# A two-layer hybrid decoder on one core: the experts' results added to the rows of x by an adding indirect DMA, weights split a whole expert ahead, no combine

## The chip, the core and the metric

The kernel runs on one core of one Trainium2 chip. A core has the engines TensorE (PE), VectorE (DVE), ScalarE (ACT), GpSimd (POOL) and SyncE (SP), an on-chip memory of 128 partitions, the matrix engine's accumulators (PSUM, 8 banks), and 16 DMA engines that move data between the chip's main memory (DRAM) and the on-chip memory. Each engine works through its own list of instructions and waits for others by semaphores. The metric is the device time of one execution in microseconds (us).

## The reference

A token is a row of 1024 numbers, and there are 2048 of them. Layer 0 mixes tokens by gated linear attention, layer 1 by a recurrent block. After each mixer comes the mixture of experts, which is what the change is about:

```python
def hier_moe(x, norm_w, w_group, w_expert, w_gate, w_up, w_down):
    h = rmsnorm(x, norm_w).reshape(n_tok, d)
    # best group of 4, then the best 2 of its 8 experts; weights of the two
    ...
    weights = p_g[:, None] * top_p
    eid = g_sel[:, None] * MOE_EXPERTS_PER_GROUP + top_e
    ...
    def expert_block(args):        # a block: up to 128 rows of one expert
        xblk, e = args
        return (jax.nn.silu(xblk @ w_gate[e]) * (xblk @ w_up[e])) @ w_down[e]
    yb = lax.map(expert_block, (xb, blk_eid)).reshape(n_rows, d)
    yb = yb * buf_w[:, None].astype(yb.dtype)
    out = jnp.zeros((n_tok + 1, d), yb.dtype).at[buf_tok].add(yb)[:n_tok]

def reference(x, ...):
    for layer in range(DEPTH):
        x = x + gla_mixer(...)  if layer % 2 == 0 else x + rglru_mixer(...)
        x = x + hier_moe(...)
    return rmsnorm(x, final_norm)
```

There are 32 experts of size 1024 x 256 (gate), 1024 x 256 (up) and 256 x 1024 (down), all fp32, so 3 MB of weights for each expert and layer.

## The kernel before

The program runs seven stages one after the other, with a barrier between them: `gla` (mixer of layer 0), `project_and_route` (output projection, residual, norm, choice of experts), `experts`, `lru` (mixer of layer 1), `project_and_route`, `experts`, `finish` (last norm).

Every large product is made of three matmuls in a 32-bit format with a shorter mantissa (`matmul3`, L118 to L120): the operands are split into a high part (`hi`, made by a copy on ACT) and a low part (`lo`, raw minus high, a subtraction of two operands on DVE or POOL). So each weight of each expert has to be split before PE can use it.

**Routing** writes for every pair of token and chosen expert the token's number into `gather_lists` by an indirect DMA (L920). It keeps the pair's weight (`k.weight`) and, after the last tile, computes at which row of `y_rows` the pair's result will stand (`k.row`, L1097 to L1103).

**Experts** walks over 32 experts, and for each over its blocks of 128 rows (`expert_blocks`). The counts are data: an expert has 1 or 2 blocks here, once 3. All engines walk the same loops. For block g, of expert e:

- POOL gathers the rows of the *next* block from `h_rows` by one indirect DMA of 512 KB (`gather`, L1274 and L1277), once the rows of block g have been transposed.
- PE multiplies by gate and up (24 matmuls of 512 columns, `experts_gu`), transposes the next block's rows (L1411), does the down product of the block *before* (`down`, 12 matmuls), and transposes the activations (L1446).
- ACT takes silu (L1346), then `hT_hi` of the next rows (L1316), y of the block before (L1323), `aT_hi` (L1350), and stores y to `y_rows` by a plain DMA (L1328).
- DVE does act = silu x up (L1397), `hT_lo` (L1386) and `aT_lo` (L1400).

Between experts stands the splitting of weights, in two slots of raw, hi and lo. At the head of expert e, ACT makes `gu_hi` of expert e+1 (L1309, 3/8 and 5/8 apart), DVE makes `wd_hi` and `wd_lo` of expert e (L1375, L1377) and 3/8 of `gu_lo` of expert e+1 (L1366), and POOL makes the other 5/8 of `gu_lo`, of expert e itself (L1285). SP loads gate and up of expert e+2 when both parts of `gu_lo` of e are done, and down of e+2 when `wd_lo` of e is done (L1241).

**The combine** stands in the stage behind. `lru` (before its norm) and `finish` gather for each of 16 tiles of tokens two rows of `y_rows` per token by indirect DMAs, `y_a` and `y_b` (L1647; L1477), and DVE adds them to x with their weights in two instructions (L1763, L1765; L1494, L1496). `lru` stores the new x again (L1589). Its SP queue holds in this order: x of tiles 0 and 1, gain, weights, store of x 0, x 2, more weights, eight small loads of parameters (L1606, L1608), then store and load of the further tiles. During `gla`, POOL sets the unused part of `y_rows` to zero by 8 DMAs of 2 MB (L418).

## Time and profile before

| | us |
|---|---|
| median of 3 runs (3321.96 to 3325.31) | 3324.17 |
| the profiled execution | 3325.53 |
| its span in the trace | 3324.0 |
| `gla` and first routing, 0 to 1156 | 1156 |
| `experts` of layer 0, 1156 to 1767 | 611 |
| `lru`, 1767 to 2338 | 571 |
| second routing, 2338 to 2619 | 281 |
| `experts` of layer 1, 2619 to 3202 | 583 |
| `finish`, 3202 to 3324 | 122 |

The stages were cut where SP issues the first load of the next one. The trace gives for each engine when an instruction ran and what ended the engine's idle time before it. The granted clock is TensorE's, 1.00 for 2.4 GHz and 0.50 for 1.2 GHz. A DMA's landing time runs from its issue to its completion.

### The profile page before, as it was taken

To read this page: it belongs to the slowest core of one execution; us is meant where nothing else is said; L and a number is where in the kernel's file an instruction comes from. 1 tells how busy PE (TensorE), PEld (TensorE's weight loads), DVE (VectorE), ACT (ScalarE), POOL (GpSimd) and SP (SyncE) were. 2 spreads that over 40 slices of the span, in tenths; PEclk is the share of its full clock that TensorE was granted. 3 is DMA by queue.
4 is the path that set the end of the run, shared out by engine and by line. 5 is a ranking of instruction groups with operands and counts; after the bars stand their busy time and mean duration, and the time that the engine had idled before them with its cause. 6 is when DMAs were issued, how large, how long until landed. Compare 5 with 4: busy or idle time off the path is not lost. (4 is left out here: it accounts for less than half of the span.)

```text
span 3324.0 us, 46214 instructions
## 1 busy us (share of the span) xinstructions
PE 2699.6 (81%) x12218; PEld 2149.8 (65%) x12219; DVE 1897.1 (57%) x3349; ACT 1505.0 (45%) x2058; POOL 706.0 (21%) x458
## 2 busy tenths in 40 slices
PE   4999969999699577988883999998799378999840
PEld 3777747777587466766762877776577356777630
DVE  3444434444366567456554788876466687544745
ACT  3444544455344244444443676675344344444423
POOL 0000000000011245344441010000011354344532
PEclk8999979999899789999996999999899698999975
DMA  3122212222444287777757455431543487777757
GB/s 109 64 70 70 76 63 70 70 76 76 151 146 132 87 284 272 266 256 259 263 197 235 147 181 161 144 120 51 191 136 126 160 294 278 263 264 252 265 205 256
DMA packets 360028, 563.86 MB, mean 170 GB/s; under 512 B 30608, under 2 KB 272416, under 8 KB 359968
## 3 DMA queue, kind: packets, MB, share of 16 engines
q1 hardware_dynamic: 314080, 402.11, 37.1%
q0 software_dynamic: 29616, 101.76, 9.1%
q10 hardware_dynamic: 16272, 59.25, 4.4%
q8 instruction: 30, 0.49, 0.1%
q14 instruction: 30, 0.25, 0.0%
HBM read 427.77 MB, written 135.30 MB: 169 GB/s over the span
## 5 line engine op out<-in xcount | busy, mean ns | idle before, releaser
L1285 POOL TENSOR_TENSOR experts_gu_lo<-experts_gu_raw,experts_gu_hi x64 | 385.6, 6025 | 160.5 <-ACT experts_gu_hi L1309 159.9
L118 PE MATMUL experts_ps<-experts_gu_hi,experts_hT_hi 128*128 (+1 forms) x760 | 331.8, 437 | 91.4 <-issue 71.3
L119 PE MATMUL experts_ps<-experts_gu_lo,experts_hT_hi 128*128 (+1 forms) x760 | 319.7, 421 | 0.0
L120 PE MATMUL experts_ps<-experts_gu_hi,experts_hT_lo 128*128 (+1 forms) x760 | 318.0, 418 | 0.0
L1366 DVE TENSOR_TENSOR experts_gu_lo<-experts_gu_raw,experts_gu_hi (+1 forms) x64 | 279.7, 4371 | 67.0 <-ACT experts_gu_hi L1309 67.0
L1309 ACT ACTIVATE experts_gu_hi<-experts_gu_raw (+1 forms) x128 | 238.0, 1908 | 91.3 <-DMA experts_gu_raw<-in_moe_w_up 32.1
L118 PE MATMUL route_ps<-route_w_hi,route_src_hi 128*128 128x512 f32 x512 | 215.1, 420 | 56.8 <-DVE route_w_lo L979 56.8
L118 PEld LDWEIGHTS experts_ps<-experts_gu_hi,experts_hT_hi 128*128 128x128 f32 x760 | 156.1, 205 | 141.0 <-issue 106.9
L118 PE MATMUL gla_ps<-gla_wvg_hi,gla_hT_hi 128*128 128x512 f32 x512 | 212.6, 415 | 0.0
L120 PE MATMUL route_ps<-route_w_hi,route_src_lo 128*128 128x512 f32 x512 | 208.7, 408 | 0.0
L119 PE MATMUL route_ps<-route_w_lo,route_src_hi 128*128 128x512 f32 x512 | 208.6, 407 | 0.0
L120 PE MATMUL gla_ps<-gla_wvg_hi,gla_hT_lo 128*128 128x512 f32 x512 | 202.5, 395 | 0.0
L119 PE MATMUL gla_ps<-gla_wvg_lo,gla_hT_hi 128*128 128x512 f32 x512 | 201.2, 393 | 0.0
L1323 ACT ACTIVATE experts_y<-experts_ps 128x1024 f32<-128x1024 f32 x97 | 99.6, 1026 | 179.2 <-PE experts_ps L120 162.9
L120 PEld LDWEIGHTS experts_ps<-experts_gu_hi,experts_hT_lo 128*128 128x128 f32 x760 | 155.0, 204 | 38.7
L119 PEld LDWEIGHTS experts_ps<-experts_gu_lo,experts_hT_hi 128*128 128x128 f32 x760 | 156.3, 206 | 33.9
L418 POOL DMA_DIRECT2D y_rows<-gla_zeros x8 | 9.2, 1146 | 787.0 <-DVE gla_tile_decay L629 787.0
L1346 ACT ACTIVATE experts_silu<-experts_ps 128x256 f32<-128x256 f32 x95 | 36.4, 383 | 292.1 <-PE experts_ps L120 290.5
L920 POOL DMA_INDIRECT gather_lists<-route_tok,route_place_int x64 | 61.8, 965 | 489.7 <-DVE route_place_int L1049 480.0
L118 PE MATMUL experts_ps<-experts_wd_hi,experts_aT_hi 128*128 (+1 forms) x388 | 161.6, 417 | 3.4 <-DVE experts_aT_lo L1400 3.4
L1411 PE MATMUL experts_ps<-ident,experts_rows 128*128 128x128 f32 x776 | 104.5, 278 | 66.6 <-DMA experts_rows<-h_rows,experts_ids_now 66.1
L119 PE MATMUL experts_ps<-experts_wd_lo,experts_aT_hi 128*128 (+1 forms) x388 | 153.3, 395 | 0.0
(311 smaller groups left out, 6571.4 us busy)
## 6 DMA issues: line engine op xcount, KB each, us to landing
experts_gu_raw<-in_moe_w_gate SPq DMA_DIRECT2D x64, 1024.0 KB, 5.7
experts_gu_raw<-in_moe_w_up SPq DMA_DIRECT2D x64, 1024.0 KB, 10.8
experts_wd_raw<-in_moe_w_down SPq DMA_DIRECT2D x64, 1024.0 KB
y_rows<-experts_y ACTq DMA_DIRECT2D x97, 512.0 KB, 6.3
gla_w_raw<-in_gla_w_in SPq DMA_DIRECT2D x18, 1024.0 KB
y_rows<-gla_zeros POOLq DMA_DIRECT2D x8, 2048.0 KB, 8.4
route_src<-oT_rows SPq DMA_DIRECT2D x32, 512.0 KB, 4.3
x_rows<-route_x_new SPq DMA_DIRECT2D x32, 512.0 KB, 2.9
```

The costliest lines, as they stand in the source:

```text
L118: nc.tensor.matmul(out, w_hi, x_hi, start=first, stop=False)
L119: nc.tensor.matmul(out, w_hi, x_lo, start=False, stop=False)
L120: return nc.tensor.matmul(out, w_lo, x_hi, start=False, stop=last)
L418: pool.dma_start(y_unused[bass.ds(n * rows, rows), :] .rearrange("(p n) (a c) -> p (n a) c", p=P, c=DV), zeros[:].unsqueeze(1).to_broadcas ...
L920: pool.indirect_dma_start(ids_out, bass.IndirectOffsetOnAxis(place_int[:, j, c:c + 1].bitcast(U32), 0), tok[:, j:j + 1], None).then_inc(sc ...
L1285: pool.tensor_tensor(gu_lo[:, slot(e), DVE_SHARE:], gu_raw[:, slot(e), DVE_SHARE:], gu_hi[:, slot(e), DVE_SHARE:].bitcast(F32), ALU.subtract)\
L1309: nc.scalar.activation(gu_hi[:, slot(e), at], gu_raw[:, slot(e), at], ACT.Copy)\
L1323: nc.scalar.activation(y[:].rearrange("p (b c) -> p b c", b=2), ps[:, Y:Y + 2], ACT.Copy)\
L1346: nc.scalar.activation(silu[:], ps[:, GU, 0:FF], ACT.Silu).then_inc(silu_done, 1)
L1366: nc.vector.tensor_tensor(gu_lo[:, slot(e), 0:DVE_SHARE], gu_raw[:, slot(e), 0:DVE_SHARE], gu_hi[:, slot(e), 0:DVE_SHARE].bitcast(F32), AL ...
L1411: last = nc.tensor.transpose(ps[:, HT_ + c // 4, (c % 4) * P:(c % 4 + 1) * P], rows[:, c * P:(c + 1) * P], k.ident[:])
```

## The change

Routing now writes entries of two numbers, the token and its weight (`entry`), into `expert_lists`. Empty places hold the numbers T to T+127, which are spare rows at the end of x. `k.row`, `k.weight` and the instructions behind them are gone, h is stored as two halves of 512 columns, and the zeroing in `gla` is gone.

In `experts` POOL splits no weights any more. DVE subtracts all of `gu_lo` of expert e+1, in four parts of 128 x 1024 that follow four parts of `gu_hi` on ACT, and `wd_lo`; ACT makes `wd_hi` too, once the down product before has ended. The rows of a block come in two gathers of 512 columns, each transposed between halves of the gate-and-up product. y is multiplied by its weight when ACT takes it from PSUM, and POOL adds it to the rows of x in DRAM by an indirect DMA with an addition (`add_y`); the next y, in the same single buffer, waits for that DMA to have landed. ACT's order within a block is now aT, y, half of hT, silu, half of hT. y has two blocks of delay to its gather, and the pipeline is filled by two dummy blocks of zeros. `lru` and `finish` read the finished x; their gathers, their combine and `lru`'s stores of x are gone.

```diff
@@ experts, POOL
             def gather(column, g):
-                pool.wait_ge(hT_ps_done, nth(g - 1))
+                for b in range(2):
+                    if not (isinstance(g, int) and g == 0):
+                        pool.wait_ge(rows_in[b], nth_dma(g - 1))
+                    stand(pool)
+                    pool.tensor_copy(source_now[b][:], sources[:, bass.ds(column, 1)]).then_inc(source_set[b], 1)
+                    pool.wait_ge(source_set[b], nth(g))
+                    pool.wait_ge(hT_ps_done, nth(2 * g - 2 + b))
+                    stand(pool)
+                    pool.indirect_dma_start(rows[:, b], None, h_halves[b],
+                                            bass.IndirectOffsetOnAxis(source_now[b][:].bitcast(U32), 0))\
+                        .then_inc(rows_in[b], DMA)
...
+            def add_y(i):
+                if not (isinstance(i, int) and i < 0):
+                    pool.wait_ge(y_added, nth_added(i - 1))
+                pool.wait_ge(listed, nth(i - 2))
                 stand(pool)
+                pool.tensor_copy(target_now[:].unsqueeze(1), by_block[:, bass.ds(i + (LAG - 2), 1), 0:1])\
+                    .then_inc(target_set, 1)
+                pool.wait_ge(target_set, nth(i + 1))
+                pool.wait_ge(y_done, nth(i))
                 stand(pool)
+                pool.indirect_dma_start(x_rows, bass.IndirectOffsetOnAxis(target_now[:].bitcast(U32), 0),
+                                        y[:], None, compute_op=ALU.add).then_inc(y_added, DMA)
-            def split_gu(e):
-                pool.wait_ge(gu_hi_done, nth(2 * e))
-                pool.tensor_tensor(gu_lo[:, slot(e), DVE_SHARE:], gu_raw[:, slot(e), DVE_SHARE:],
-                                   gu_hi[:, slot(e), DVE_SHARE:].bitcast(F32), ALU.subtract)\
-                    .then_inc(gu_lo2_done, 1)
@@ experts, ACT
+            def take_y(i):
+                act.wait_ge(y_ps_done, nth(i))
+                act.wait_ge(y_added, nth_added(i - 1))
+                act.wait_ge(listed, nth(i - 2))
+                stand(act)
+                nc.scalar.activation(y[:].rearrange("p (b c) -> p b c", b=2), ps[:, Y:Y + 2], ACT.Copy,
+                                     scale=by_block[:, bass.ds(i + (LAG - 2), 1), 1].bitcast(F32))\
+                    .then_inc(y_done, 1)
...
+            def before(e, first):
+                if not is_last(e):
+                    split_gu(e + 1)
+                split_wd(e, first)
             def each(e, b, g):
+                take_aT(g)
+                take_y(g)
+                take_rows(g + 1, 0)
                 act.wait_ge(gu_ps_done, nth(g))
                 act.wait_ge(act_done, nth(g - 1))
                 nc.scalar.activation(silu[:], ps[:, GU, 0:FF], ACT.Silu).then_inc(silu_done, 1)
-                take_rows(g + 1)
-                take_y(g)
-                act.wait_ge(aT_ps_done, nth(g))
-                nc.scalar.activation(aT_hi[:], ps[:, AT, 0:FF].rearrange("p (a c) -> p a c", c=P), ACT.Copy)\
-                    .then_inc(aT_hi_done, 1)
-                store_y(g)
+                take_rows(g + 1, 1)
@@ experts, PE
             def each(e, b, g):
-                pe.wait_ge(gu_lo_done, nth(e))
-                pe.wait_ge(gu_lo2_done, nth(e))
-                pe.wait_ge(hT_lo_done, nth(g))
                 pe.wait_ge(act_done, nth(g - 1))
...
+                for half in range(2):
+                    pe.wait_ge(hT_lo_done, nth(2 * g + half))
+                    for c in range(KD)[of_half(half)]:
+                        if c % PK == 0:
+                            pe.wait_ge(gu_lo_done, nth(PARTS * e + c // PK))
+                        last = matmul3(nc, ps[:, GU], hT_hi[:, c], hT_lo[:, c], gu_hi[:, slot(e), c],
+                                       gu_lo[:, slot(e), c], c == 0, c == KD - 1)
+                    if half == 1:
+                        last.then_inc(gu_ps_done, 1)
+                    transpose_rows(g + 1, half)
@@ lru (finish in the same way)
-            def combine(t):
-                j = t % 2
-                after_dma(dve, x_in[j], t // 2)
-                after_dma(dve, y_in[j], 2 * (t // 2) + 1)
-                step(nc.vector.scalar_tensor_tensor(out=x[:, j], in0=y_a[:, j], scalar=k.weight[:, t, 0:1],
-                                                    in1=x[:, j], op0=ALU.mult, op1=ALU.add))
-                nc.vector.scalar_tensor_tensor(out=x[:, j], in0=y_b[:, j], scalar=k.weight[:, t, 1:2],
-                                               in1=x[:, j], op0=ALU.mult, op1=ALU.add).then_inc(x_done, 1)
```

POOL's list in the loop over experts (experts 0 to 30), in the kernel before: first what stands once per expert, then one block, whose loop is closed by L1216.

```order
L1285 TENSOR_TENSOR experts_gu_lo<-experts_gu_raw,experts_gu_hi 128x2560
...
L1214 TENSOR_LOAD block_at
...
L1215 TENSOR_LOAD blocks
...
L1274 COPY experts_ids_now<-experts_ids 128x1
...
L1277 DMA experts_rows<-h_rows,experts_ids_now 128x1024
L1216 REGISTER_ALU
L1216 COMPARE_AND_BRANCH
```

The same place in the changed kernel:

```order
L1194 TENSOR_LOAD block_at
...
L1195 TENSOR_LOAD blocks
...
L1267 COPY experts_source_now<-experts_sources 128x1
...
L1271 DMA experts_rows<-h_rows,experts_source_now 128x512
L1267 COPY experts_source_now<-experts_sources 128x1
...
L1271 DMA experts_rows<-h_rows,experts_source_now 128x512
...
L1275 COPY experts_by_block<-experts_lists 128x2
...
L1282 COPY experts_target_now<-experts_by_block 128x1
...
L1287 DMA x_rows<-experts_y,experts_target_now 2176x1024
```

The subtraction of weights has left POOL. A block now has three DMAs and four small copies there in place of one and one, and the adding DMA stands behind both gathers.

ACT's list in the same loop, in the kernel before, with the weights of the next expert first and one block behind them:

```order
L1309 ACTIVATE experts_gu_hi<-experts_gu_raw 128x2560
...
L1309 ACTIVATE experts_gu_hi<-experts_gu_raw 128x1536
...
L1346 ACTIVATE experts_silu<-experts_ps 128x256
...
L1316 ACTIVATE experts_hT_hi<-experts_ps 128x512 x2
...
L1323 ACTIVATE experts_y<-experts_ps 128x1024
L1350 ACTIVATE experts_aT_hi<-experts_ps 128x256
...
L1328 DMA y_rows<-experts_y 128x1024
```

The same place in the changed kernel, from the last of the four parts of `gu_hi` on:

```order
L1335 ACTIVATE experts_gu_hi<-experts_gu_raw 128x1024
...
L1342 ACTIVATE experts_wd_hi<-experts_wd_raw 128x2048
...
L1318 ACTIVATE experts_aT_hi<-experts_ps 128x256
...
L1326 ACTIVATE experts_y<-experts_ps,experts_by_block 128x1024
...
L1313 ACTIVATE experts_hT_hi<-experts_ps 128x512
...
L1363 ACTIVATE experts_silu<-experts_ps 128x256
...
L1313 ACTIVATE experts_hT_hi<-experts_ps 128x512
```

`wd_hi` has come to ACT, the store of y has left it, and y is taken ahead of silu.

## Rows read from the trace of the kernel before

**Rows 1.** Stretches: each engine's busy us (instructions), granted clock, DMA share, GB/s.
```profile
1156.00:1767.00 611.00, 510.07 (x2274) 402.00 (x2274) 348.43 (x294) 258.32 (x314) 271.30 (x134) 0.92 0.73 251
1767.00:2338.00 571.00, 478.51 (x2048) 382.32 (x2048) 426.98 (x472) 345.44 (x391) 49.14 (x50) 0.92 0.46 149
```

**Rows 2.** Timeline of ACT: start and length in us of each block's silu.
```profile
1185.37 0.38 ACT L1346 ACTIVATE experts_silu<-experts_ps 128x256 f32<-128x256 f32 x1 [1.46 <-PE experts_ps L120]
1194.85 0.38 ACT L1346 ACTIVATE experts_silu<-experts_ps 128x256 f32<-128x256 f32 x1 [4.48 <-PE experts_ps L120]
...
1224.59 0.38 ACT L1346 ACTIVATE experts_silu<-experts_ps 128x256 f32<-128x256 f32 x1
1243.37 0.38 ACT L1346 ACTIVATE experts_silu<-experts_ps 128x256 f32<-128x256 f32 x1 [6.04 <-PE experts_ps L120]
...
1754.31 0.38 ACT L1346 ACTIVATE experts_silu<-experts_ps 128x256 f32<-128x256 f32 x1 [4.49 <-PE experts_ps L120]
...
2649.22 0.39 ACT L1346 ACTIVATE experts_silu<-experts_ps 128x256 f32<-128x256 f32 x1 [1.90 <-PE experts_ps L120]
...
3151.16 0.38 ACT L1346 ACTIVATE experts_silu<-experts_ps 128x256 f32<-128x256 f32 x1 [0.21 <-PE experts_ps L120]
3169.28 0.38 ACT L1346 ACTIVATE experts_silu<-experts_ps 128x256 f32<-128x256 f32 x1 [5.46 <-PE experts_ps L120]
...
3188.25 0.38 ACT L1346 ACTIVATE experts_silu<-experts_ps 128x256 f32<-128x256 f32 x1 [4.50 <-PE experts_ps L120]
```

**Rows 3.** Timeline inside one long interval, on POOL, DVE and PE.
```profile
1223.49 6.26 POOL L1285 TENSOR_TENSOR experts_gu_lo<-experts_gu_raw,experts_gu_hi  x1 [5.30 <-ACT experts_gu_hi L1309]
1229.70 1.71 POOL L1274 COPY experts_ids_now<-experts_ids 128x1 int32 x1
1232.20 0.98 POOL L1277 DMA_INDIRECT experts_rows<-h_rows,experts_ids_now  x1 [0.79 <-POOL experts_ids_now L1274]
...
1224.72 6.65 DVE L1366 TENSOR_TENSOR experts_gu_lo<-experts_gu_raw,experts_gu_hi  x1 [0.49 <-ACT experts_gu_hi L1309]
...
1235.09 0.79 PE L118 MATMUL experts_ps<-experts_gu_hi,experts_hT_hi 128*128 x1 [2.89 <-issue]
```

**Rows 4.** Timeline, one `gu_lo` on DVE; then groups of 1156 to 1767.
```profile
1331.63 1.76 DVE L1366 TENSOR_TENSOR experts_gu_lo<-experts_gu_raw,experts_gu_hi  x1 [0.37 <-ACT experts_gu_hi L1309]
...
L1309 ACT ACTIVATE experts_gu_hi<-experts_gu_raw x62 | 115.3, 1908 | 41.1 <-DMA experts_gu_raw<-in_moe_w_gate 16.0 <-issue 15.3 <-DMA experts_gu_raw<-in_moe_w_up 9.8
L1377 DVE TENSOR_TENSOR experts_wd_lo<-experts_wd_raw,experts_wd_hi x31 | 71.1, 2293 | 3.8
```

**Rows 5.** DMA of 1156 to 1767: queues with share, then issues, us to landing.
```profile
q1 hardware_dynamic: 75408, 100.93, 50.2%
q0 software_dynamic: 7200, 26.22, 12.5%
q10 hardware_dynamic: 7200, 26.22, 10.5%
...
y_rows<-experts_y ACTq DMA_DIRECT2D x50, 512.0 KB, 6.2
experts_rows<-h_rows,experts_ids_now POOLq DMA_INDIRECT x50, 7.5
```

**Rows 6.** Timeline of `lru`: load of x 3, first large matmul.
```profile
1805.60 0.34 SPq L1585 DMA_DIRECT2D lru_x<-x_rows  x1
...
1821.91 0.80 PE L118 MATMUL lru_ps<-lru_hT_hi,lru_wx_hi 128*128 128x512 f32 x1 [4.29 <-DVE lru_hT_lo L1779]
```

**Rows 7.** Timeline of `finish`: from one tile to the next.
```profile
3281.68 0.16 DVE L1491 COPY finish_weight_now<-weight 128x2 f32 x1
...
3284.60 1.06 ACT L247 ACTIVATE finish_square<-finish_x 128x1024 f32<-128x1024 f32 x1 [4.35 <-DVE finish_x L1496]
...
3290.48 1.06 ACT L247 ACTIVATE finish_square<-finish_x 128x1024 f32<-128x1024 f32 x1 [4.35 <-DVE finish_x L1496]
```

**Rows 8.** One tile's view in `lru`: ns min/median/max of the gather's issue.
```profile
L1647 POOL DMA_INDIRECT lru_y_a<-y_rows,lru_row_now x16: 957/1833/1842, 1768.4 to 2110.7; - x16
```

More of the change, by code:

```diff
@@ L1295, in next_rows @@
                     gather(nc.s_assert_within(column, min_val=0, max_val=E * SLOTS - 1), g + 1)
+                    add_y(g)
                 return next_rows
             gather(0, 0)
-            blocks = expert_blocks(pool, None, split_gu, each)
-            pool.wait_ge(rows_in, nth_dma(blocks))
+            add_y(-1)
+            blocks = expert_blocks(pool, None, None, each)
+            for i in range(2):
+                add_y(blocks + i)
+            for b in range(2):
+                pool.wait_ge(rows_in[b], nth_dma(blocks))
@@ L1320, in take_y @@
-            def take_y(g):
-                act.wait_ge(y_ps_done, nth(g))
-                act.wait_ge(y_stored, nth_store(g - 1))
-                nc.scalar.activation(y[:].rearrange("p (b c) -> p b c", b=2), ps[:, Y:Y + 2], ACT.Copy)\
-                    .then_inc(y_done, 1)
-            def store_y(g):
-                act.wait_ge(y_done, nth(g))
-                act.dma_start(y_rows[bass.ds(g * P, P), :], y[:]).then_inc(y_stored, DMA)
+                for c in range(PARTS):
+                    stand(act)
+                    nc.scalar.activation(gu_hi[:, slot(e), of_part(c)], gu_raw[:, slot(e), of_part(c)], ACT.Copy)\
+                        .then_inc(gu_hi_done, 1)
@@ L1330, in _, with split_wd @@
+            def split_wd(e, first):
+                act.wait_ge(wd_in, nth_dma(e))
+                act.wait_ge(y_ps_done, nth(first))
+                stand(act)
+                nc.scalar.activation(wd_hi[:, slot(e)], wd_raw[:, slot(e)], ACT.Copy).then_inc(wd_hi_done, 1)
             act.wait_ge(zeroed, 1)
@@ L1403, in _ @@
-            expert_blocks(dve, each, before)
+                take_rows(g + 1, 1)
+            blocks = expert_blocks(dve, each, before)
+            take_aT(blocks)
         @block.tensor
         def _(pe):
-            def transpose_rows(g):
-                pe.wait_ge(rows_in, nth_dma(g))
-                pe.wait_ge(hT_lo_done, nth(g - 1))
-                for c in range(KD):
-                    last = nc.tensor.transpose(ps[:, HT_ + c // 4, (c % 4) * P:(c % 4 + 1) * P],
-                                               rows[:, c * P:(c + 1) * P], k.ident[:])
-                last.then_inc(hT_ps_done, 1)
@@ L1431, in each @@
+            down(0, 1)
+            transpose_act(0)
             def each(e, b, g):
-                pe.wait_ge(gu_lo_done, nth(e))
-                pe.wait_ge(gu_lo2_done, nth(e))
-                pe.wait_ge(hT_lo_done, nth(g))
                 pe.wait_ge(act_done, nth(g - 1))
-                for c in range(KD):
-                    last = matmul3(nc, ps[:, GU], hT_hi[:, c], hT_lo[:, c], gu_hi[:, slot(e), c],
-                                   gu_lo[:, slot(e), c], c == 0, c == KD - 1)
-                last.then_inc(gu_ps_done, 1)
@@ L1636, in _ @@
             after_dma(sp, y_stored, STEPS - 1)
-            for j in range(2):
-                after_dma(sp, x_stored[j], NT // 2 - 1)
-        @block.gpsimd
-        def _(pool):
-            for t in range(NT):
-                after(pool, x_done, t - 2)
-                pool.tensor_copy(row_now[:, t % 2], k.row[:, t]).then_inc(row_set, 1)
-                after(pool, row_set, t)
-                for c, rows in enumerate((y_a, y_b)):
-                    pool.indirect_dma_start(rows[:, t % 2], None, y_rows,
-                                            bass.IndirectOffsetOnAxis(row_now[:, t % 2, c:c + 1].bitcast(U32), 0))\
-                        .then_inc(y_in[t % 2], DMA)
         @block.scalar
@@ L1657, in mean_square @@
             def mean_square(t):
-                after(act, x_done, t)
+                after_dma(act, x_in[t % 2], t // 2)
                 after(act, std_done, t - 1)
@@ L1922, in lru, with finish @@
         m.end()
-def finish(nc, k, x_dram, y_rows, norm_w, out):
+def finish(nc, k, x_dram, norm_w, out):
     DEPTH = 4
@@ L1932, in finish @@
         square = m.sb("square", [P, D])
-        y_a, y_b = m.sb("y_a", [P, DEPTH, D]), m.sb("y_b", [P, DEPTH, D])
-        cb = Combine(m, k, x, h, square[:], y_a, y_b, DEPTH)
+        norm = Norm(m, k, x, h, square[:], DEPTH)
+        x_in = [m.plain(f"x_in{j}") for j in range(DEPTH)]
         stored = [m.store(f"stored{j}") for j in range(DEPTH)]
```

380 lines of the change are left out of this document (165 added, 215 removed).

## Prediction

> **What bounds the kernel now.** I read the stretches first, one per stage, because the bound differs from stage to stage. In `experts` of layer 0 PE is busy 510 of 611 us and DMA 0.73 of the time; in `lru` PE is busy 479 of 571 [rows 1]. So both wait mainly for PE, and the question is where PE loses its rest. The next view is the timeline of ACT's silu, which comes once per block and so ticks the blocks. The 49 blocks of layer 0 and the 46 of layer 1 make 48 + 45 = 93 intervals, of together 568.9 + 539.0 = 1108.0 us [rows 2]. Inside an expert of two blocks an interval is 9.48 us. But 22 intervals (11 in each layer, the first 18.78 us, the last 18.12 us) take 399.3 us together, 18.15 each; the other 71 have a mean of 9.98 [rows 2].
>
> The timeline inside one long interval shows why. POOL's part of `gu_lo` takes 6.26 us and DVE's 6.65 us, both at once, where DVE alone needs 1.76 us for the same [rows 3, 4]. DVE's act for PE is queued behind that instruction, and so are `hT_lo` and `aT_lo`. PE starts the next block after another 2.89 us of idle, with a matmul of 0.79 us, a length that stands where the granted clock is 0.50 [rows 3]. It happens behind an expert of one block, when the weights of two experts are split close together. Layer 0 has 15 such experts and layer 1 has 19 (counted from silus between two `gu_hi`).
>
> **The change part by part**, against the profiled execution's 3325.5 us (1.4 above the median).
>
> *The port stalls go.* POOL subtracts no more, so the 22 long intervals lose their cause. What is late next in a block of an expert of one block is DVE or ACT. DVE: `gu_lo` is twice the size of `wd_lo`, 4.6 us, plus 2.3 for `wd_lo` [rows 4], plus what a block costs it, some 2 us (act, `aT_lo`, `hT_lo`; estimated from ACT's 2.8 below, which has y in it), is 8.9. ACT: two instructions of 1.91 for `gu_hi`, half of them again for `wd_hi`, 5.7 in all; a block costs (258.3 - 32 x 3.8) / 49 = 2.8 us; together 8.5 [rows 1, 4]. Each has about ten waits and two register loads around that. I take 10.4 us for such a block and 9.7 for the others, where PE sets the pace. With 34 blocks of experts of one block and 59 other intervals this floor is 34 x 10.4 + 59 x 9.7 = 926 us, 182 less than 1108.
>
> *A new loop of waits comes.* y has one buffer. ACT may take the next y only when the adding DMA of the last has landed, and POOL may issue that only when ACT has written y. Queued behind ACT's wait are half of hT, silu and the other half of hT; behind POOL's wait are both gathers of the next block. So a block can't be shorter than landing time L of the adding DMA, plus y on ACT (1.0, half as many columns as a mean `gu_hi` of 1.91 [rows 4]) and the semaphores between (0.6). Nothing in the trace is an adding DMA. From below, L is at least that of the plain store of y, 6.2 us, plus 0.6 for POOL's longer issue: 6.8. From above it is a gather and a store in series, 7.5 + 6.2 - 0.3 = 13.4 [rows 5]. I take **9.0**, nearer to the store, because it moves the same rows to the same memory and the read in front is spread over 16 engines and pipelined row by row; the gather, which is a read with POOL's issue, is only 0.7 above the store so counted. Then the loop is 10.6 us, for every block.
>
> In experts of one block DVE is busy nearly throughout with two-input subtractions. POOL's copy took 1.71 us behind one of them [rows 3], for one number per partition, and a gather's issue took 1.83 us at the median against 0.96 at the least while DVE was busy in `lru` [rows 8]. I add 1.0 us to the loop there: 11.6. The blocks then take 34 x 11.6 + 59 x 10.6 = 1020 us, **88 less**. With L = 6.8 the floor holds, 182 less; with 13.4 they take 34 x 16.0 + 59 x 15.0 = 1429, 321 more. Each us of L is 93 us of time.
>
> *DMA.* Per layer the queues hold the 16 engines for 0.502 + 0.125 + 0.105 = 0.732 of 611 us, 447 us [rows 5]. The store of y (64 us) becomes the add. If its read of x costs as much again it is 511 us of a stage that I expect to last some 570. That is under the stage, so the sum takes nothing for it beyond L. The Trainium skill, "Collectives: The Full Stack", section "The bandwidth ceiling", says that an add in the DMA engines runs at half the rate of a copy, for the two reads and not for the addition. By that rule the 64 us double, as in the bound above; no row here shows it.
>
> *The rows in halves.* Two issues and two copies more on POOL, about 6.2 us of POOL per block, inside 10.6: three times an issue of 0.98, 0.79 before it [rows 3] and a copy of some 0.2, and one copy more. The first half can start when half of the rows is transposed. The waits for rows that lengthen some of the 71 ordinary intervals go; they are inside the 9.7 above. Cost nothing, hidden by the loop; if POOL falls behind, see the rivals.
>
> *Head and tail of `experts`.* Two more POOL fills, a list of twice the size and a dummy add delay the first gather; the 6 us of DVE beside POOL at the head go. I take +2 each (-5 to +6). At the end the stage runs 12.7 us from the last silu at 1754.31 to 1767 [rows 1, 2], with one store. Now the last y but one can stand one loop after silu, and the last y a second, shorter one (the engines' queues empty, L some 6.5), and its add lands 6.5 later: 9 + 8 + 6, 10 more, or less where the loop isn't full: +9 each (+6 to +14). Both layers: **+22**.
>
> *`lru`.* The first large matmul starts at 1821.91, 54 us into the stage. It waits for tile 3, whose x was issued only at 1805.60 [rows 6], as SP waited with the store of x 1 behind eight small loads, and tile 0 waited for its two gathers. Now x 0 lands some 5 us into the stage, h of tile 0 is there about 10 us earlier, SP goes through the small loads 14 us earlier, and DVE saves two combines of 2.6 behind x 3: **-18** (-10 to -25). In the steady part DVE loses 2.6 us in 11 of 16 steps, but PE sets the pace there, so 0 (bound: -22, the time in which PE waited for `hT_lo`).
>
> *`finish`.* A tile takes 3290.48 - 3284.60 = 5.88 us, a serial chain over DVE and ACT. The combine in it lasts from 3281.68 to 3284.60, 2.92 us [rows 7]. What replaces it is ACT's own issue of the output before the next square, 0.6 us. So 3.6 us per tile, 15 times 2.3 is 34 less; the start loses the two gathers and one combine, about 12 less, and the end 3 less: **-49** (-40 to -56). DMA then moves 1 MB in 3.6 us, 290 GB/s, more than the mean of 251 in `experts` [rows 1], so a little may come back.
>
> *Routing and `gla`.* The row computation at its end (3 us of DVE) stands beside the last scatter's landing; the zeroing of 16 MB runs beside PE. **-2** (0 to -8).
>
> Sum: -88 + 22 - 18 - 49 - 2 = -135, so 3325.5 - 135 = **3190 us**. With L from 8 to 10 the blocks take 34 x 10.6 + 59 x 9.7 = 933 (175 less) to 34 x 12.6 + 59 x 11.6 = 1113 (5 more), so 3103 to 3283.
>
> **Rivals.**
> *Series add (slower).* The adding DMA reads x, waits, then writes, and with three streams in the engines' queues each part waits again. Break-even is where the blocks take 47 us more, L = 10.5. Past that it is slower; at L = 11.5 the blocks take 34 x 14.1 + 59 x 13.1 = 1252, +144, total 3423. For: both parts stand in the loop, and the store alone is 6.2 [rows 5]. Against: rows go through independently. 0.18.
> *All hidden.* L stays under 8, blocks run at the floor of 926: -182 + 22 - 69 = -229, 3096. 0.13.
> *DMA is the bound.* The add doubles its engine time and 511 us of each layer run at a share of 0.92, so 556 us plus a head of 25 where little moves, 581 in place of 611. Layer 1 in proportion: 59 less for both, and the rest -69: 3197. For: 0.73 is a mean over stretches with none [rows 1]. Against: 511 still fits. It gives nearly the forecast's time by another way. 0.10.
> *The port fight moves.* DVE's four parts block each of POOL's seven small steps by one part, 1.2 us. POOL needs 6.2 + 8.4 = 14.6 in a block of an expert of one block, so 34 x 14.6 + 59 x 10.6 = 1122, +14, and with the rest 3292; the splitting ahead then gains nothing. For: the copy of 1.71 [rows 3]. The Trainium skill, "SBUF — State Buffer", section "SBUF: two separate sides", says that a DVE instruction with two on-chip inputs and a POOL instruction that reads there exclude each other for their whole length. The 6.65 against 1.76 agrees. By it POOL's copies are the ones that wait. 0.09.
>
> **How the numbers follow.** Forecast 0.50. Faster: 0.50 + 0.13 + 0.10 + 0.07 of the last = 0.80. Slower: 0.17, from the series add. The rest, 0.03, lies within 0.2% (6.6 us, about what a measurement can tell here). The range leaves out a twentieth below 3085 and some 0.14 above 3340, the far part of the series add.
>
> **What would show it.** In the trace after: no `gu_lo` of 6 us; silu intervals of 10 to 11 us without a second cluster at 18; the add's landing 8 to 10 us; ACT's y waiting for a DMA and no more for PE; `finish` tiles of 3.6 us; the first large matmul of `lru` 36 us into its stage. Wrong if L is over 10.5, if intervals of one-block experts stay above 14, or if DMA share is at 0.95 all through.

## The result, and the profile after

| | before | after |
|---|---|---|
| device time, median (us) | 3324.17 | 3337.06 (3331.00 to 3343.38) |
| profiled execution (us) | 3325.5 | 3335.0 |
| granted clock, whole span | 0.905 | 0.926 |

The ratio is 1.0040, with a 95% interval from 1.0024 to 1.0056: slightly slower, where 3190 us was forecast. First four of the stages, as in [rows 1]: start, end and length in us, then the busy us (instructions) of PE, its weight loads, DVE, ACT and POOL, the granted clock, the DMA share and GB/s.

```profile
1153.00:1807.00 654.00, 511.12 (x2288) 398.62 (x2288) 324.69 (x360) 327.53 (x412) 267.03 (x360) 0.94 0.81 237
1807.00:2356.00 549.00, 479.75 (x2048) 381.63 (x2048) 387.29 (x440) 345.33 (x391) 1.39 (x3) 0.94 0.34 109
2633.00:3254.00 621.00, 490.11 (x2150) 381.81 (x2150) 317.29 (x348) 317.43 (x396) 251.76 (x336) 0.93 0.82 244
3254.00:3333.30 79.30, 0.00 (x0) 0.00 (x0) 23.18 (x32) 33.35 (x56) 0.00 (x0) 0.50 0.65 218
```

The rows are `experts` of layer 0, `lru`, `experts` of layer 1 and `finish`. `lru` went from 571 [rows 1] to 549 us. `experts` of layer 0 went from 611 to 654, although PE is busy there for the same 511 us. So the stages outside `experts` gained, 72 us together, and `experts` took back 81. The silus, which tick the blocks as in [rows 2], first and last of each layer:

```profile
1186.46 0.39 ACT L1363 ACTIVATE experts_silu<-experts_ps 128x256 f32<-128x256 f32 x1
1783.05 0.38 ACT L1363 ACTIVATE experts_silu<-experts_ps 128x256 f32<-128x256 f32 x1 [2.27 <-PE experts_ps L119]
...
2663.43 0.39 ACT L1363 ACTIVATE experts_silu<-experts_ps 128x256 f32<-128x256 f32 x1
3228.79 0.38 ACT L1363 ACTIVATE experts_silu<-experts_ps 128x256 f32<-128x256 f32 x1 [2.27 <-PE experts_ps L119]
```

The 93 intervals are 596.6 + 565.4 = 1162.0 us, where they were 1108.0 [rows 2] and 1020 was forecast. The 18 us cluster is gone but for one of 19.2. Now the interval behind an expert's first block is long, 13.2 us on average in an expert of one block and 13.8 in one of two, and that behind a second block is 10.4. The groups of the whole program show what PE, ACT and POOL wait for (busy us, mean ns | idle before, releasers):

```profile
L1427 PE MATMUL experts_ps<-ident,experts_rows 128*128 128x128 f32 x776 | 125.1, 286 | 170.7 <-DMA experts_rows<-h_rows,experts_source_now 170.7
L1287 POOL DMA_INDIRECT x_rows<-experts_y,experts_target_now x101 | 182.0, 1802 | 307.3 <-ACT experts_y L1326 292.2 <-POOL experts_target_now L1282 8.9 <-issue 6.2
L1326 ACT ACTIVATE experts_y<-experts_ps,experts_by_block 128x1024 f32<-128x1024 f32 x99 | 109.9, 1110 | 155.8 <-DMA x_rows<-experts_y,experts_target_now 155.7
L117 PE MATMUL experts_ps<-experts_wd_hi,experts_aT_hi 128*128 (+1 forms) x396 | 169.0, 427 | 52.4 <-DVE experts_aT_lo L1394 47.9 <-ACT experts_y L1326 3.7 <-issue 0.8
```

PE's first wait is for the gathered rows, 170.7 us; the same group of before had 66.6. POOL stands 292.2 us in front of the adding DMA, waiting for ACT's y. Two turns of the chain in layer 0, ACT, POOL and PE (start, length in us):

```profile
1431.27 3.90 ACT L1335 ACTIVATE experts_gu_hi<-experts_gu_raw  x4 [2.14 <-DMA experts_gu_raw<-in_moe_w_up]
1435.07 1.90 ACT L1342 ACTIVATE experts_wd_hi<-experts_wd_raw  x1
...
1437.14 1.11 ACT L1326 ACTIVATE experts_y<-experts_ps,experts_by_block 128x1024 f32<-128x1024 f32 x1
...
1441.01 3.90 ACT L1335 ACTIVATE experts_gu_hi<-experts_gu_raw  x4 [1.41 <-issue]
1444.82 1.90 ACT L1342 ACTIVATE experts_wd_hi<-experts_wd_raw  x1
...
1448.60 1.12 ACT L1326 ACTIVATE experts_y<-experts_ps,experts_by_block 128x1024 f32<-128x1024 f32 x1 [1.62 <-DMA x_rows<-experts_y,experts_target_now]
...
1439.06 2.00 POOL L1287 DMA_INDIRECT x_rows<-experts_y,experts_target_now  x1 [5.16 <-ACT experts_y L1326]
...
1442.59 1.91 POOL L1271 DMA_INDIRECT experts_rows<-h_rows,experts_source_now  x1 [0.90 <-POOL experts_source_now L1267]
...
1450.55 1.64 POOL L1287 DMA_INDIRECT x_rows<-experts_y,experts_target_now  x1 [1.22 <-ACT experts_y L1326]
...
1453.30 1.02 POOL L1271 DMA_INDIRECT experts_rows<-h_rows,experts_source_now  x1 [0.91 <-POOL experts_source_now L1267]
...
1460.50 0.18 POOL L1282 COPY experts_target_now<-experts_by_block 128x1 int32 x1 [3.94 <-DMA x_rows<-experts_y,experts_target_now]
...
1449.47 0.65 PE L1427 MATMUL experts_ps<-ident,experts_rows 128*128 128x128 f32 x4 [1.70 <-DMA experts_rows<-h_rows,experts_source_now]
...
1461.27 0.65 PE L1427 MATMUL experts_ps<-ident,experts_rows 128*128 128x128 f32 x4 [2.09 <-DMA experts_rows<-h_rows,experts_source_now]
```

In the first turn ACT splits weights until 1436.97, so y starts only at 1437.14. POOL has stood 5.16 us for it. Its gather of the next rows, 1442.59, stands behind the add, and PE idles for 1.70 us until those rows land. In the second turn the splits end at 1446.72, but y starts only at 1448.60, when the add of 1439.06 has landed. Here the forecast's own loop over the single buffer holds y. The add, the gather (1453.30) and PE (2.09 us of idle) follow as before. So a y that is late behind the splits delays its add, and by the landing the next y too. The second add lands 1460.50 - 1450.55 = 9.95 us after its issue begins; over 36 adds in 1190 to 1700 whose landing something waited for, the mean is 9.12.

### The profile page after: what moved, and what is told of

Its sections match the earlier page's. It is cut to its first block and busy times, and to the rows that moved or that the text cites. A ratio compares the mean times of both kernels' runs of the same rounds, so it can differ in the third digit from the quotient of the medians.

```text
span 3333.3 us, 48901 instructions
## 1 busy us (share of the span) xinstructions
PE 2704.1 (81%) x12246; PEld 2143.8 (64%) x12247; DVE 1745.7 (52%) x3359; ACT 1641.2 (49%) x2254; POOL 591.7 (18%) x796
## 3 DMA queue, kind: packets, MB, share of 16 engines
q0 software_dynamic: 32688, 105.99, 12.7%
## 5 line engine op out<-in xcount | busy, mean ns | idle before, releaser
L1377 DVE TENSOR_TENSOR experts_gu_lo<-experts_gu_raw,experts_gu_hi (+1 forms) x256 | 296.6, 1220 | 161.2 <-ACT experts_gu_hi L1335 155.4
L117 PE MATMUL experts_ps<-experts_gu_hi,experts_hT_hi 128*128 (+1 forms) x760 | 331.2, 436 | 43.3 <-issue 31.9
L1335 ACT ACTIVATE experts_gu_hi<-experts_gu_raw (+1 forms) x256 | 249.8, 1047 | 133.2 <-DMA experts_gu_raw<-in_moe_w_up 87.5
L1427 PE MATMUL experts_ps<-ident,experts_rows 128*128 128x128 f32 x776 | 125.1, 286 | 170.7 <-DMA experts_rows<-h_rows,experts_source_now 170.7
L1389 DVE TENSOR_TENSOR experts_hT_lo<-experts_ps,experts_hT_hi 128x512 fp32r<-128x512 f32 x194 | 133.1, 687 | 198.2 <-ACT experts_hT_hi L1313 195.3
L1287 POOL DMA_INDIRECT x_rows<-experts_y,experts_target_now x101 | 182.0, 1802 | 307.3 <-ACT experts_y L1326 292.2
L1427 PEld LDWEIGHTS experts_ps<-ident,experts_rows 128*128 128x128 f32 x776 | 96.1, 146 | 215.6 <-issue 198.3
L1271 POOL DMA_INDIRECT experts_rows<-h_rows,experts_source_now x194 | 201.0, 1036 | 177.1 <-POOL experts_source_now L1267 129.2
L117 PE MATMUL experts_ps<-experts_wd_hi,experts_aT_hi 128*128 (+1 forms) x396 | 169.0, 427 | 52.4 <-DVE experts_aT_lo L1394 47.9
L1326 ACT ACTIVATE experts_y<-experts_ps,experts_by_block 128x1024 f32<-128x1024 f32 x99 | 109.9, 1110 | 155.8 <-DMA x_rows<-experts_y,experts_target_now 155.7
```

Source lines behind the costliest of these rows:

```text
L117: nc.tensor.matmul(out, w_hi, x_hi, start=first, stop=False)
L1271: pool.indirect_dma_start(rows[:, b], None, h_halves[b], bass.IndirectOffsetOnAxis(source_now[b][:].bitcast(U32), 0))\
L1287: pool.indirect_dma_start(x_rows, bass.IndirectOffsetOnAxis(target_now[:].bitcast(U32), 0), y[:], None, compute_op=ALU.add).then_inc(y_add ...
L1326: nc.scalar.activation(y[:].rearrange("p (b c) -> p b c", b=2), ps[:, Y:Y + 2], ACT.Copy, scale=by_block[:, bass.ds(i + (LAG - 2), 1), 1]. ...
L1335: nc.scalar.activation(gu_hi[:, slot(e), of_part(c)], gu_raw[:, slot(e), of_part(c)], ACT.Copy)\
L1377: nc.vector.tensor_tensor(gu_lo[:, slot(e), of_part(c)], gu_raw[:, slot(e), of_part(c)], gu_hi[:, slot(e), of_part(c)].bitcast(F32), ALU.s ...
```

## Experiments

Theory A is the forecast's own: the loop over the single y (landing, y, issue) sets the block's time, with y late on ACT behind the weight splits. Its rivals are B, the 16 DMA engines, and C, the weight splits on ACT and DVE. D came after the first four runs: POOL's wait for y holds up the next block's gathers, which stand behind it on POOL.

One table for all. "Layer 0" is the sum of the 48 intervals of layer 0, where every kernel has the same 49 blocks; "rows" is PE's idle time for rows over the program. The kernel before was run beside each group: 3322.7, 3320.4 and 3323.1 us.

| kernel | us | ratio to before (95%) | layer 0 | rows |
|---|---|---|---|---|
| before | 3324.2 | | 568.9 | 66.6 |
| after | 3337.1 | 1.0040 (1.0024 to 1.0056) | 596.6 | 170.7 |
| two_y | 3345.1 | 1.0056 (1.0035 to 1.0077) | 605.7 | 189.8 |
| y_first | 3331.7 | 1.0023 (1.0013 to 1.0032) | 595.1 | 48.4 |
| two_y_first | 3315.8 | 0.9976 (0.9964 to 0.9987) | 586.0 | 64.1 |
| no_add | 3246.6 | 0.9770 (0.9754 to 0.9786) | 555.4 | 119.5 |
| no_add_free | 3139.2 | 0.9453 (0.9437 to 0.9469) | 507.2 | 47.1 |
| two_y_lag | 3226.5 | 0.9713 (0.9695 to 0.9732) | 525.3 | 63.1 |
| among | 3266.0 | 0.9831 (0.9815 to 0.9847) | 559.2 | 79.3 |
| among_lag | 3243.5 | 0.9763 (0.9747 to 0.9780) | 539.1 | 55.8 |
| no_loads | 3205.3 | 0.9640 (0.9624 to 0.9656) | 532.3 | 49.1 |
| write_rows | 3249.1 | 0.9775 (0.9758 to 0.9791) | 560.5 | 114.1 |
| one_gather_lag | 3298.8 | 0.9921 (0.9899 to 0.9944) | 566.0 | 138.6 |
| between_lag | 3241.0 | 0.9743 (0.9726 to 0.9760) | 533.6 | 91.4 |

### two_y: a second buffer for y

```diff
-        y = m.sb("y", [P, D])
+        y = m.sb("y", [P, 2, D])
...
-                act.wait_ge(y_added, nth_added(i - 1))
+                act.wait_ge(y_added, nth_added(i - 2))
```

> The changed kernel with two buffers for y: ACT may write y of the next block while the adding DMA of the last is on its way; POOL still issues one add only when the one before has landed. It chooses between two written-out issues by the parity of the block. Theory A (the loop y, issue, landing on one buffer sets the block's time, with y late on ACT behind the weight splits): the loop shrinks to landing 9.0, the copy of the target and the issue, some 10 us, blocks take 10.6 instead of 12.4, 93 x 1.8 = 167 less, total about 3170 (3140 to 3230). Rival B (the 16 DMA engines are the limit: doubled add, share 0.81): bytes and landings stay, so no more than 20 less, 3317 or above. Rival C (the splits of weights on ACT and DVE are the limit): no more than 20 less too, but then ACT's y would not have waited for a DMA in half of the blocks.

It is no faster than after. ACT's wait for the add's DMA is gone:

```profile
L1337 ACT ACTIVATE experts_y<-experts_ps,experts_by_block 128x1024 f32 x99 | 109.6, 1107 | 10.2 <-PE experts_ps L119 7.3
L1438 PE MATMUL experts_ps<-ident,experts_rows 128*128 128x128 f32 x776 | 127.2, 290 | 189.8 <-DMA experts_rows<-h_rows,experts_source_now 189.8
```

So 145 us of ACT's waiting could be taken away and nothing came of it. But the buffer takes away only ACT's part of the loop. In `add_y` POOL itself waits until the last add has landed before it copies the next targets, and that wait stayed (207.9 us here, 209.7 in after):

```profile
L1286 POOL COPY experts_target_now<-experts_by_block 128x1 int32 (+1 forms) x101 | 53.0, 525 | 208.3 <-DMA x_rows<-experts_y,experts_target_now 207.9 <-issue 0.2
```

So this run shows that ACT's wait on the one buffer does not set the block's time. It does not show that the landing has no part in it. B and C both survive.

### y_first and two_y_first: ACT's aT and y ahead of the splits

```diff
 def each(e, b, g):
-    take_aT(g)
-    take_y(g)
     take_rows(g + 1, 0)
...
     take_rows(g + 1, 1)
+    take_aT(g + 1)
+    take_y(g + 1)
```

> The changed kernel with one y buffer, but ACT takes aT and y at the end of a block (and DVE the low part of aT), so ahead of the weight splits that stand at the next expert's head. Theory A: the loop is then landing 9.0 + y 1.11 + 0.88 to the issue = 11.0 and no longer 12.4, so up to 93 x 1.4 = 130 less; some of it is lost because hT and silu now stand behind the splits alone: 3215 to 3270. Rival B (DMA engines): within 15 of 3337. Rival C (splits are the limit): within 15 of 3337, or slower since y's wait now stands before the splits.

> Both: two buffers for y and ACT's aT and y ahead of the splits. Theory A: what is left is POOL's own chain of adds, 9.0 + about 0.8, against PE's 9.7, so blocks of 10.0 to 10.4 and a total of 3110 to 3150, below each of the two alone. Rival B: within 20 of 3337. Rival C: not below two_y alone.

y_first gains next to nothing, as both rivals had it, but its waits changed places:

```profile
L1427 PE MATMUL experts_ps<-ident,experts_rows 128*128 128x128 f32 x776 | 120.7, 280 | 48.4 <-DMA experts_rows<-h_rows,experts_source_now 48.2
L1435 PE MATMUL experts_ps<-ident,experts_act 128*128 128x128 f32 x194 | 41.1, 295 | 94.7 <-DVE experts_act L1415 94.7
```

PE's idle time for rows fell from 170.7 to 48.4 when y came early. That hints that the rows had been late because of y, but it is no proof: POOL still waits 269.3 us for y, and a PE that comes late for another reason waits less for rows. What was won came back as 94.7 us for DVE's act, since silu and act now stand behind the splits, and as 31.9 to 74.0 us of "issue" in front of `gu`. Theory A missed the two runs by 62 and 166 us. They pointed at POOL: the only link from y to the gathers is POOL's program order.

### no_add and no_add_free: without adding, and without POOL's wait for y

```diff
                 pool.wait_ge(target_set, nth(i + 1))
-                pool.wait_ge(y_done, nth(i))
-                stand(pool)
-                pool.indirect_dma_start(x_rows, ..., y[:], None, compute_op=ALU.add).then_inc(y_added, DMA)
```

no_add keeps the wait for `y_done`; no_add_free leaves it out too. The waits for `y_added` go in both.

> The changed kernel with the adding DMA left out (y is computed but never added to x, so the output is the residual path alone) and with it all waits for its landing; POOL still copies the target and waits for y. Everything else stands. Theory A: blocks fall to the floor of 9.7 to 10.4, 93 x 2.3 = 214 less, and 15 more at head and tail: about 3110. Rival B (DMA engines): the same, as 138 us of engine time go per layer, so this run alone does not tell A from B; it bounds what all of adding costs. Rival C: blocks stay at 12 or more, 3280 or above.

> As no_add (the adding DMA and the waits for it left out, so y is never added to x), and POOL's wait for y is left out as well: nothing holds POOL between the gathers of one block and those of the next. Theory D, formed on the first runs (POOL's wait for y, which ACT writes behind the weight splits, holds up the next block's gathers): PE's waits for rows, 35 us in layer 0 of no_add, go to near 0, and the total falls by 50 to 70 from 3247, to about 3185. Rival C (the weight splits on ACT and DVE alone set the long blocks): within 15 of 3247.

With no add at all the time is 3246.6 and not 3110. Leaving out one more wait on POOL, with no DMA behind it, takes 107 us more:

```profile
L1420 PE MATMUL experts_ps<-ident,experts_rows 128*128 128x128 f32 x784 | 119.0, 275 | 47.1 <-DMA experts_rows<-h_rows,experts_source_now 47.1
L1271 POOL DMA_INDIRECT experts_rows<-h_rows,experts_source_now x196 | 217.7, 1111 | 408.4 <-PE experts_ps L1420 314.7 <-DMA experts_rows<-h_rows,experts_source_now 57.0 <-POOL experts_source_now L1267 36.6
```

Now POOL waits for PE (314.7 us) and not PE for POOL. Theory D holds, and by more than it expected. Both kernels have the same blocks; in layer 0 alone the step is 555.4 to 507.2. Against after, no_add saves 91 us with POOL's wait for y still in place (a little more, block for block, as it has one block more in layer 1). So the landing had a price too, and the wait for y one of its own.

### two_y_lag: the whole work, with POOL's add one block later

```diff
                     gather(nc.s_assert_within(column, ...), g + 1)
-                    add_y(g)
+                    add_y(g - 1)
```

On top of two_y; nothing is left out.

> two_y, and POOL issues each add one block later, when its y has long been written, so that POOL never waits for ACT's y, only for the add before. Theory D: PE's waits for rows, 63 us in layer 0 of two_y, go to near 0; some of it comes back as waits for DVE's parts behind the splits, so 60 to 100 less than two_y's 3345: 3245 to 3285. Rival A (the loop over y, now over two blocks) and rival B (DMA engines): within 20 of 3345.

3226.5 us, 119 less than two_y and 94 less than before, from the place of one call (the list of targets is one block longer for it). It beats every other complete kernel here.

```profile
L1436 PE MATMUL experts_ps<-ident,experts_rows 128*128 128x128 f32 x776 | 119.6, 278 | 63.1 <-DMA experts_rows<-h_rows,experts_source_now 62.9
L1278 POOL DMA_INDIRECT x_rows<-experts_y,experts_target_now x103 | 188.8, 1833 | 124.1 <-issue 108.6 <-ACT experts_y L1335 11.9 <-POOL experts_target_now L1286 3.7
L117 PE MATMUL experts_ps<-experts_wd_hi,experts_aT_hi 128*128 (+1 forms) x396 | 173.4, 438 | 84.5 <-DVE experts_aT_lo L1403 81.0 <-ACT experts_y L1335 3.5
```

POOL's wait for y is down from 292.2 (after) to 11.9 us, and PE's for rows from 170.7 to 63.1. POOL's wait for the landing is still in the code, but falls from 207.9 (two_y) to 61.4 us, since the adds are no longer issued late. The next bound may be the DMA engines: in 1200 to 1700 us their share is 0.94, where after has 0.84, and ACT waits 115 us for weights, where it waits 88 in after. No run takes the loads out of two_y_lag, so this is not shown. Theory C alone is out for after, as the splits are still in one piece here; they are what makes y late.

```profile
1200.00:1700.00 500.00, 452.61 (x2102) 356.94 (x2101) 300.92 (x333) 301.18 (x380) 263.56 (x320) 0.99 0.94 278
```

### among, among_lag and between_lag: the splits spread over a block

```diff
 def each(e, b, g):
+    with act.If(b < 1):
+        if not is_last(e):
+            split_gu(e + 1, range(0, 2))
+        take_rows(g + 1, 0)
+        if not is_last(e):
+            split_gu(e + 1, range(2, 4))
+        take_gu(g)
+        take_rows(g + 1, 1)
+        split_wd(e, g)
```

`take_gu` is the silu with its waits; DVE has the same with its third and fourth part around act. between_lag takes only aT, on both engines, between `split_gu` and `split_wd`.

> y_first, and the weight splits of an expert are no longer one piece at the head of its first block: on ACT and DVE the parts of gate and up stand before hT, between hT and silu, and wd after the second hT, with a branch on the block's number that skips them elsewhere. One y buffer. Theory C (in y_first and two_y_first the splits in one piece make each first block 12.0 to 15): first blocks fall to 11.0, where landing 9.0 + y 1.1 + 0.9 holds them (theory A's loop), 34 + 28 first blocks win about 1.5: 80 less than y_first's 3332, 3250. Rival B (DMA engines): one-block experts stay at 13 to 15 and the total within 25 of 3332.

> among with two buffers for y and POOL's adds one block later. If all of A, C and D hold, blocks fall to PE's own 9.5 to 10.4 and the total to 3150 to 3190. Rival B (DMA engines): per layer the engines hold 0.81 of 654 = 530 us, so a stage can't be below some 555 and one-block experts not below 14 us each; the total stays above 3190 and the weights are what ACT waits for.

> two_y_lag (3226.5), and in an expert's first block ACT and DVE take aT between the split of gate and up and that of wd, in place of behind both (a branch on the block's number). PE's waits for DVE's aT_lo, 28 us in layer 0 of two_y_lag, should go: if theory C's rest (splits in one piece ahead of aT) is what is left of the 11.6 us blocks, 30 to 50 less, 3180 to 3200. If the branch costs as much, or the DMA engines (share above 0.8) now set the one-block experts: within 20 of 3226.

With one y buffer the spreading is worth 3331.7 - 3266.0 = 66 us over y_first, so the splits in one piece held that order up (theory C, for y_first). With POOL freed it is worth nothing: among_lag and between_lag are 17 and 15 us slower than two_y_lag, where 3150 to 3190 and 3180 to 3200 were hoped for. In between_lag PE's wait for DVE's aT_lo is gone, but ACT's y (32.2 us) and "issue" before `gu` (54.7, from 21.5) came in its place. Whether that is the branches or the DMA engines, I did not separate.

### no_loads and write_rows: what the DMA engines have to do with it

```diff
-            with sp.Fori(0, E - 2) as e:
-                ...
-                load_gu(e + 2)
-                ...
-                load_wd(e + 2)
```

> The changed kernel, but only the weights of the first two experts of each layer are loaded; the 30 others reuse them (so from the third expert on the output is made with wrong weights). All instructions of the engines stay, the queues lose 94 of 101 MB per layer. Theory D (POOL's wait for y, behind ACT's splits, holds up the gathers): the chain stays and only its two landings shorten, add from 9.0 to some 7 and rows likewise, so blocks lose about 1 us: 3337 - 93 = about 3245 (3200 to 3290). Rival B (the DMA engines set the blocks): blocks fall to PE's 9.5 to 10.4 and the total under 3160.

```diff
-                                        y[:], None, compute_op=ALU.add).then_inc(y_added, DMA)
+                                        y[:], None).then_inc(y_added, DMA)
```

> The changed kernel with the indirect DMA writing y over the rows of x in place of adding to them (so x loses its residual and the first expert's part; the second layer's routing changes with it). What an add costs over a write of the same rows by the same queue: its read. If the add's engine time is doubled by that read (q0 holds the engines for 214 us in layer 0, some 76 of it gathers), q0 falls to about 145 us, landing from 9.0 to 7.5, and the total by 93 x 1 or so, to 3240 (3220 to 3290). If the landing is set by POOL's issue and the queue and not by the read: landing within 0.5 of 9.0 and total within 30 of 3337. The number of blocks in layer 1 may differ; layer 0 is the comparison.

Only the weights of the first two experts are loaded; the others reuse them. The adds then land after 6.78 us (12 of them), not 9.12, and the total falls to 3205, not under 3160: shorter landings within the same chain, near the lower end of what theory D expected (3200 to 3290). Some 11 us of it are a block less in layer 1; layer 0 falls by 64. POOL still waits 323.6 us for y. B is thus no rival for after, but the loads lengthen the DMA links of the chain: PE's wait for rows is 49.1 us without the loads.

Writing in place of adding lands after 8.21 us (25 of them) and saves 88 us. For 0.91 us less of landing that is near the forecast's 93 us per us of it. Engine time per DMA, from queue 0 in 1200 to 1700 us: a half gather 0.142 x 500 / 92 = 0.77 us (no_add_free), a write (0.240 x 500 - 85 x 0.77) / 42 = 1.30, an add (0.396 x 500 - 91 x 0.77) / 46 = 2.78 (two_y_lag). POOL's issue of an add is longer too, 1802 ns against 1184 (mean). So the addition costs 1.5 us of the engines per block but only 0.9 of landing time, 0.6 of which is POOL's longer issue. This rests on one kernel each.

### one_gather_lag: are the halves worth their issues?

```diff
-                for b in range(2):
+                for b in range(1):
...
-                    pool.wait_ge(hT_ps_done, nth(2 * g - 2 + b))
+                    pool.wait_ge(hT_ps_done, nth(2 * g - 1))
```

On top of two_y_lag; the gather takes whole rows, from one tensor in place of two.

> two_y_lag (3226.5) with one gather of whole rows per block in place of two of half rows, as before the change: one copy and one issue less on POOL, but the gather starts only when both halves are transposed and PE's first transpose waits for all of it. If the halves bring what the prediction let them bring (the waits for rows go): undoing them costs 93 x 1 to 2 us, 3310 to 3400. If POOL's extra issues cost as much as the halves gain: within 25 of 3226.

The cost is 72 us, a little under the 84 at which the expected range began, and PE's wait for rows goes from 63.1 to 138.6. The halves earn their issues: the first half's rows can be on their way some 3 us earlier (in two_y_lag ACT takes the halves of one block's hT at 1426.09 and 1429.32).

## Why the prediction was wrong

*The sign and the total.* Forecast 3190, measured 3337.06, near the top of the range (3085 to 3340) and in the case of 0.17, slower. But the number and the sign were met by none of the rivals: the floor was not reached, the add isn't in series (9.12 us, break-even was 10.5), and the DMA share is not 0.92 throughout. The port fight had 14.6 us behind a block of an expert of one block. It came as 13.2, with 8 of 32 above the 14 that was named as a sign of being wrong; in two_y_lag, with the same parts on DVE and the same steps on POOL, it is 12.0, so the fight did not hold it. That 3337 lies within the range is luck of its width.

*The port stalls go: right.* No `gu_lo` of 6 us is left (four parts, together 4.6), and the second cluster at 18 us is gone, as the forecast named it. (The 34 blocks of experts of one block are 33: in the order of `wd_hi` and silu layer 1 has 18 of them and none of three blocks, which changes the sum by 1 us.)

*The landing: right.* L was taken as 9.0 and is 9.12, between 7.4 and 10.0. y took 1.1 for 1.0, and from y's end to the add's issue 0.8 for 0.6. Loop by these: 11.1 for 10.6.

*The step that failed* is "Cost nothing, hidden by the loop; if POOL falls behind, see the rivals", in the part on the rows in halves, together with "they are inside the 9.7". The text had said one part earlier that both gathers of the next block stand behind POOL's wait, and then gave it no price. The loop was costed as if it closed at y, with y ready when the landing comes. It goes on: splits 5.8 us on ACT, y, the add, two copies and issues, the rows' landing of some 7 to 8, PE. Each link was in the rows or in the code. Priced, it is: PE's waits for rows in after are 170.7 us, and were 66.6 before. The sum of the intervals was forecast as 1020 and came as 1162. By kind the intervals came as 13.2 us (32 of them) behind a block of an expert of one block, for 11.6; 13.8 (31) behind the first of two blocks, for 10.6; and 10.4 (30) behind the second, for 10.6. Two thirds of the miss thus stand behind first blocks of two, for which the forecast added nothing. In two_y_lag these are 12.0, 11.2 and 10.2, and the sum is 525.3 + 512.3 = 1037.6, 18 off. The later add, with the second buffer that it needs, gives back 124 of the 142 us that were missing.

*The loop as bound: right in part.* Only half of the y's (25 of 49 in layer 0) waited for a DMA, and two_y, which ends ACT's wait and leaves POOL's, gained nothing. So the loop was not the bound of every block. But it was no mere bystander: it carries a late y on into the next block, write_rows saves 88 us for 0.91 us of L (0.6 of it POOL's shorter issue), and no_add, with POOL's wait for y still there, 91. no_loads takes 2.3 us off the landing, gathers are shorter too, and 132 us go, 11 of them with the block less. No run has the order of after with the landing alone changed.

*Head and tail of experts: right in kind, short in size.* The head of layer 0 is 1186.46 - 1153 = 33.5 (29.4 before), the tail 1807 - 1783.05 = 24 (12.7 before). That is 15 in layer 0 and, by the same reading, 12 in layer 1, together 27 for the 22 forecast.

*DMA.* Doubled engine time was the bound for the add, and it came, and a little more: q0 had 12.5% of 611 us and q10 10.5% [rows 5], together 141; now queue 0 has 214 of 654.

```profile
q1 hardware_dynamic: 75408, 101.19, 47.9%
q0 software_dynamic: 15488, 53.49, 32.8%
```

A write of 1.30 and an add of 2.78 us per block (above) are 2.1 times. The Trainium skill, "Collectives: The Full Stack", section "The bandwidth ceiling", has the add at half a copy's rate for its two reads; these runs agree. The sum "takes nothing for it beyond L". No run gives the price of that engine time apart from the landing's.

*The port, after the change.* POOL's copy took 0.19 us alone and up to 2.53 behind DVE's parts (two_y_lag, 1437.11), and its issues 1.0 against 1.9 (after, 1442.59). The 1.0 us per block set aside for that was the right kind of number; no run prices it alone.

*lru: right.* -22 for -18; the first large matmul starts 31.5 us after the stage's first load, for 36 forecast and 54 before.

```profile
1808.47 0.83 SPq L1561 DMA_DIRECT2D lru_x<-x_rows  x2
...
1840.02 0.79 PE L117 MATMUL lru_ps<-lru_hT_hi,lru_wx_hi 128*128 128x512 f32 x1 [2.01 <-DVE lru_hT_lo L1724]
```

*finish: right per tile, short at both ends.* A tile takes 3305.48 - 3301.82 = 3.66 us, for 3.6. Every fourth takes some 3 us more, with two table loads of ACT, but it did so before the change too (in the second fence), so this cancels. From the first square to the last it is 65.0 us, from 97.9: -33 for -34. The start gave 9 of 12 and the end half a us of 3. Together 79 us, from 122, is -43 for -49.

```profile
3301.82 1.06 ACT L244 ACTIVATE finish_square<-finish_x 128x1024 f32<-128x1024 f32 x1 [2.19 <-DVE finish_h L255]
...
3305.48 1.06 ACT L244 ACTIVATE finish_square<-finish_x 128x1024 f32<-128x1024 f32 x1 [2.18 <-DVE finish_h L255]
...
3313.15 1.28 ACT L244 ACT_TABLE_LOAD   x1 [2.54 <-issue]
...
3315.61 1.28 ACT L248 ACT_TABLE_LOAD   x1
```

Before the change:

```profile
3243.94 1.28 ACT L247 ACT_TABLE_LOAD   x1 [4.56 <-DVE finish_x L1496]
...
3246.46 1.28 ACT L251 ACT_TABLE_LOAD   x1
```

In all: the combine's removal gave 65 us as forecast (67), the rest of the program 7 for 2, and `experts` took 81 where 66 less was forecast.

## What to carry to other kernels

When a wait is added on an engine, write down what is queued behind it and follow that on to its consumer before giving it a price of nothing; a loop is as long as its longest way round, not the way that shares its buffer. Before calling a wait removed, look for a second instruction that waits for the same event (POOL's, in two_y). A queue that issues DMAs for two purposes, one early and one late, couples them: issue the late one a turn later, when what it waits for is long done, and give it the buffer that this needs (119 us here; the buffer alone gave nothing). And an experiment that removes all of a suspect (no_add) can still leave its queueing in place; the one that removes only the wait found the cause.

## What the hardware showed that was not expected

An indirect DMA with an addition of 128 rows of 4 KB lands 9.12 us after its issue with the weights streaming beside it, 6.78 without them; the same DMA without the addition lands after 8.21. It holds the DMA engines for 2.78 us against 1.30, and POOL for 1.8 against 1.2, so from the end of the issue the two land after 7.3 and 7.0. With the engines at a share of 0.94 the adds in two_y_lag land after 9.9 (14 of them).
